# Compression of keys and values with position columns beside raw rows, second layers among other products, and gate rows turned half a chunk later

## The reference

```
kv = (h @ w_kv).reshape(B, T, 6, 4, 64)          # h: tokens normed and modulated, T = 512
k_cmp_raw, v_cmp_raw = kv[:, :, 0], kv[:, :, 1]  # 4 groups of 64
tok = arange(31)[:, None] * 16 + arange(32)      # 31 blocks of 32 tokens, stride 16
def compress(raw, j):
    blk = raw[:, tok] + cmp_pos[j]               # cmp_pos: (2, 32, 64)
    blk = ... .reshape(B, 31, 4, 32 * 64)
    hid = gelu(blk @ cmp_w1[j] + cmp_b1[j])      # (2048 -> 256)
    return hid @ cmp_w2[j] + cmp_b2[j]           # (256 -> 64)
gates = sigmoid((h2 @ w_in)[..., 1024:])         # 48 gates a token: 16 heads x 3 branches
o = gates[0] * o_compressed + gates[1] * o_selected + gates[2] * o_window
```

## Time and profile before

| | |
|---|---|
| time, median of 3 runs | 1574.64 us |
| profiled execution, its own time | 1574.64 us |
| its span in the trace | 1572.9 us |
| PE busy | 1517.3 us (96%) |
| DVE busy | 1101.3 us (70%) |
| ACT busy | 692.1 us (44%) |
| POOL busy | 291.8 us (19%) |

### The profile page before, as it was taken

The page is one execution under the profiler, slowest core; times in us unless marked ns, Lnnn a source line. Parts: engine busy times, 40 slices in busy tenths (PEclk is TensorE's granted clock), DMA queues, the critical chain, the costliest instruction groups (busy, mean ns, idle before and its releaser), DMA issues. The chain is left out here.

```text
span 1572.9 us, 20896 instructions
## 1 busy us (share of the span) xinstructions
PE 1517.3 (96%) x8187; PEld 1258.8 (80%) x8187; DVE 1101.3 (70%) x1610; ACT 692.1 (44%) x1176; POOL 291.8 (19%) x233
## 2 busy tenths in 40 slices
PE   4999999999999999989999999999999999999998
PEld 3888888888888887867777888888888988677677
DVE  6798688889988753458884785656634815888775
ACT  3433551323224543347774632323233525877651
POOL 0200013223231000149872011111100011000210
PEclk9999999999999999999999999999999999999999
DMA  9674267577684215310001164443332232111101
GB/s 332 238 271 165 81 215 248 195 251 255 207 315 134 81 59 168 104 56 2 2 2 41 68 221 161 144 146 119 134 107 90 75 107 93 68 54 54 54 1 54
DMA packets 106744, 203.35 MB, mean 129 GB/s; under 512 B 6025, under 2 KB 11414, under 8 KB 106646
## 3 DMA queue, kind: packets, MB, share of 16 engines
q1 hardware_dynamic: 106646, 202.01, 37.6%
HBM read 199.90 MB, written 2.10 MB: 128 GB/s over the span
## 5 line engine op out<-in xcount | busy, mean ns | idle before, releaser
L727 ACT ACTIVATE WH<-RAW 128x2048 fp32r<-128x2048 f32 (+1 forms) x111 | 208.1, 1886 | 354.9 <-DMA RAW<-in_ff_w_in_dram 223.7
L1242 DVE TENSOR_TENSOR WL<-RAW,WH 128x2048 fp32r<-128x2048 f32 (+1 forms) x107 | 269.1, 2538 | 120.0 <-ACT WH L727 119.2
L491 POOL PARTITION_ALL_REDUCE MROW<-MACC x26 | 123.3, 4744 | 600.8 <-DVE MACC L1276 515.9
L2105 PE MATMUL PS<-WH,HIDh 128*128 128x512 f32 (+1 forms) x576 | 217.4, 377 | 1.1 <-DVEq L1818 1.1
L2105 PE MATMUL PS<-WL,HIDh 128*128 128x512 f32 (+1 forms) x576 | 217.3, 377 | 0.0
L2105 PE MATMUL PS<-WH,HIDl 128*128 128x512 f32 (+1 forms) x576 | 217.3, 377 | 0.0
L2105 PE MATMUL PS<-HTh,WH 128*128 128x512 f32 (+1 forms) x520 | 202.5, 389 | 0.6 <-DVE WL L1242 0.6
L2105 PE MATMUL PS<-HTl,WH 128*128 128x512 f32 (+1 forms) x520 | 202.4, 389 | 0.0
L2105 PE MATMUL PS<-HTh,WL 128*128 128x512 f32 (+1 forms) x520 | 202.3, 389 | 0.0
L1276 DVE SCALAR_TENSOR_TENSOR MACC<-MRAW,CS,MACC 128x512 f32<-128x512 f32 x168 | 126.3, 752 | 8.6 <-DMA MRAW<-in_ada_w_dram 1.1
L2062 PE MATMUL PS<-HTh,WH 128*128 128x256 f32 (+1 forms) x384 | 125.3, 326 | 6.8 <-DVE WL L1242 4.4
(11 more groups left out here) (341 smaller groups left out, 2991.4 us busy)
## 6 DMA issues: line engine op xcount, KB each, us to landing
MRAW<-in_ada_w_dram SPq DMA_DIRECT2D x44, 1024.0 KB, 7.4
RAW<-in_ff_w_in_dram SPq DMA_DIRECT2D x32, 1024.0 KB, 5.4
RAW<-in_ff_w_out_dram SPq DMA_DIRECT2D x32, 1024.0 KB, 5.1
RAW<-in_w_in_dram SPq DMA_DIRECT2D x16, 1024.0 KB, 5.4
MRAW<-in_w_ada_dram SPq DMA_DIRECT2D x12, 1024.0 KB, 8.6
RAW<-in_a_w_in_dram SPq DMA_DIRECT2D x8, 1024.0 KB, 9.9
MRAW<-in_kv_ada_w_dram SPq DMA_DIRECT2D x8, 1024.0 KB, 6.0
RAW<-in_kv_w_dram SPq DMA_DIRECT2D x6, 1024.0 KB, 5.2
```

The costliest lines, as they stand in the source:

```text
L491: pool.partition_all_reduce(MROW[:], MACC[:], P, RADD).then_inc(m_red, 1)
L727: act.activation(WH[:, wslot(u), 0:width(u)], RAW[:, u % 4, 0:width(u)], ACT.Copy).then_inc(w_hi, 1)
L1242: dve.tensor_tensor(WL[:, u % 4, 0:width(u)], RAW[:, u % 4, 0:width(u)], WH[:, wslot(u), 0:width(u)].bitcast(F32), ALU.subtract).then_inc( ...
L2105: mm = pe.matmul(po, a, b_, start=(k == 0 and i == 0), stop=(k == KT - 1 and i == len(ops) - 1), skip_group_check=len(ops) > 3)
```

## The change

- Positions are no longer added to the rows. The raw rows go to a tile RK ordered by offset within a stride (8 offsets), for each of which 128 columns (4 groups of 32) lie side by side, with one position column at each end. The first layer reads 128 columns of it (124 before) for each weight piece; the product of positions arrives in PSUM columns 0 and 128. The 16 adds on DVE and the tile RP go away.
- DVE adds the two position columns and the bias `cmp_b1` with two instructions of one column per hidden half (`hidden_bias`), and the gelu takes the sum as its bias.
- The first layer goes to banks 4 to 7, which the group before the last has freed, so it doesn't wait for group 36 to be read out.
- The order on PE becomes: keys both halves, values first half, second layer of keys, values second half, scores. The second layer of values stands behind the scores of unit 3, and its bias on DVE behind the maximum of unit 5. `vc_copies` is waited for ahead of the first turn (unit 12).
- CW1v is loaded in two DMAs of 128 columns, each with its semaphore.
- The gate rows are turned between the two halves of the next chunk. ACT rounds the next weight halves ahead of the sigmoid.

```diff
+    sb("RK_END", [P, 32])
-    R = at("R", [P, 2, GROUPS, T // 2], F32, o_rb)
+    RK = at("RK", [P, 2, 8, 130], F32, o_rb)
-    RP = at("RP", [P, 2, 2, 8, GROUPS, CMP], F32, o_hid + 16384)
@@ sync_program
-        sp.dma_start(CW1[1][:], cmp_w1[1].rearrange("(m p) n -> p m n", p=P)).then_inc(cw_in, 16)
+        for mo in range(2):
+            s = slice(P * mo, P * mo + P)
+            sp.dma_start(CW1[1][:, :, s], cmp_w1[1].rearrange("(m p) n -> p m n", p=P)[:, :, s]
+                         ).then_inc(cw1_in[mo], 16)
@@ pool_program
         pool.tensor_copy(VC[32:64, :, HD:2 * HD], VC[0:32, :, 0:HD]).then_inc(vc_copies, 1)
+        pool.wait_ge(vc_copies, 1)
@@ act_program
-        chunk(gates)
+        split_next()
+        act.wait_ge(full, 4 * n.group + 1)
+        act.activation(GROW[:], bank(n.group, 0)[0:48, :], ACT.Copy).then_inc(ev_a, 1)
+        n.group += 1
+        n.chunk += 1
+        split_next()
+        act.wait_ge(full, 4 * n.group)
+        act.activation(GT[:].rearrange("p t g -> p (t g)"), bank(n.group - 1, 1)[:, 0:TT * 48], ACT.Sigmoid
+                       ).then_inc(ev_a, 3)
...
-        chunk(halves(raw_kv))
+        chunk(halves(raw_kv), split=False)
...
             for mo in range(2):
-                act.activation(HC[:, mo, :], PS[:, 2 * j + mo, 0:GROUPS * CMP], ACT.Gelu_apprx_tanh,
-                               bias=C1[:, C_B1 + 2 * j + mo:C_B1 + 2 * j + mo + 1]).then_inc(hc_r, 1)
+                act.wait_ge(hc_b, 4 * j + 2 * mo + 2)
+                act.activation(HC[:, mo, :].rearrange("p (g c) -> p g c", c=CMP),
+                               hidden(j, mo)[:, 1:129].rearrange("p (g c) -> p g c", c=32)[:, :, 0:CMP],
+                               ACT.Gelu_apprx_tanh, bias=SM[:, 40 + 2 * j + mo:41 + 2 * j + mo]).then_inc(hc_r, 1)
@@ evict_raw
-            two = ps[HD * e:HD * e + HD, :].rearrange("p (t o) -> p o t", o=2)
+            two = ps[HD * e:HD * e + HD, :].rearrange("p (c m o) -> p o m c", m=8, o=2)
             for odd in range(2):
-                last = copy(R[HD * odd:HD * odd + HD, j, h, :], two[:, odd, :])
+                last = copy(RK[HD * odd:HD * odd + HD, j, :, 1 + 32 * h:33 + 32 * h], two[:, odd])
+    def hidden(j, mo):
+        return PS[:, 4 + 2 * j + mo, :]
@@ dve_program
...
+        def hidden_bias(j, mo):
+            ps, i = hidden(j, mo), 2 * j + mo
+            dve.wait_ge(hc_f, i + 1)
+            b = SM[:, 40 + i:41 + i]
+            dve.tensor_tensor(b, ps[:, 0:1], C1[:, C_B1 + i:C_B1 + i + 1], ALU.add).then_inc(hc_b, 1)
+            dve.wait_ge(hc_b, 2 * i + 1)
+            dve.tensor_tensor(b, ps[:, 128:129], b, ALU.add).then_inc(hc_b, 1)
+        hidden_bias(0, 0)
+        hidden_bias(0, 1)
+        hidden_bias(1, 0)
...
+        hidden_bias(1, 1)
...
+            if t == 5:
+                compressed_values()
@@ pe_program
         pe.wait_ge(t2_rdy, 16)
-        chunk("A", HIDh, HIDl)
+        chunk("A", HIDh, HIDl, between=turn_gates)
...
+        def hidden_rows(j, mo):
+            pe.wait_ge((cw0_in, cw1_in[mo])[j], 16)
+            for m in range(16):
+                half = m // 8
+                mm = pe.matmul(hidden(j, mo)[:, half:half + P], CW1[j][:, m, P * mo:P * mo + P],
+                               RK[:, j, m % 8, 2 * half:2 * half + P], start=(m == 0), stop=(m == 15),
+                               skip_group_check=True)
+            mm.then_inc(hc_f, 1)
+        evicted(35)
+        hidden_rows(0, 0)
+        hidden_rows(0, 1)
+        hidden_rows(1, 0)
+        pe.wait_ge(hc_r, 2)
+        pe.wait_ge(cw_in, 64)
...
+        hidden_rows(1, 1)
+        def compressed_values():
+            pe.wait_ge(hc_r, 4)
...
-        pe.wait_ge(kc_r, 3)
+        pe.wait_ge(kc_r, 2)
...
-        pe.wait_ge(vc_copies, 1)
         for t in range(UNITS + VALUES_LAG):
             if t < UNITS:
                 scores(t)
+            if t == 3:
+                compressed_values()
+            if t == TURN_LAG:
+                pe.wait_ge(vc_copies, 1)
```

More of the change, by code:

```diff
@@ L251, in program @@
     ln_st, ln_sd, ln_v, mix_c = sem("ln_st"), sem("ln_sd"), sem("ln_v"), sem("mix_c")
-    cw0_in = sem("cw0_in")
-    cw_in, rp_c, hc_f, hc_r, kc_f, kc_r = (sem(n) for n in (
-        "cw_in", "rp_c", "hc_full", "hc_rdy", "kc_full", "kc_rdy"))
+    cw0_in, cw1_in = sem("cw0_in"), [sem("cw1_in0"), sem("cw1_in1")]
+    cw_in, hc_f, hc_b, hc_r, kc_f, kc_r = (sem(n) for n in (
+        "cw_in", "hc_full", "hc_bias", "hc_rdy", "kc_full", "kc_rdy"))
     k_hi, k_lo, kc_full32 = sem("k_hi"), sem("k_lo"), sem("kc_full32")
@@ L998, in act_program @@
         for j in range(2):
-            act.wait_ge(hc_f, 2 * j + 2)
-            if j == 1:
-                act.wait_ge(kc_f, 1)
             for mo in range(2):
-                act.activation(HC[:, mo, :], PS[:, 2 * j + mo, 0:GROUPS * CMP], ACT.Gelu_apprx_tanh,
-                               bias=C1[:, C_B1 + 2 * j + mo:C_B1 + 2 * j + mo + 1]).then_inc(hc_r, 1)
+                act.wait_ge(hc_b, 4 * j + 2 * mo + 2)
+                act.activation(HC[:, mo, :].rearrange("p (g c) -> p g c", c=CMP),
+                               hidden(j, mo)[:, 1:129].rearrange("p (g c) -> p g c", c=32)[:, :, 0:CMP],
+                               ACT.Gelu_apprx_tanh, bias=SM[:, 40 + 2 * j + mo:41 + 2 * j + mo]).then_inc(hc_r, 1)
             if j == 0:
@@ L1007, in act_program @@
                 act.wait_ge(pool_c, 8)
-                act.activation(KCF[:, :, 0:CMP], PS[:, 4, 0:GROUPS * CMP].rearrange("p (g c) -> p g c", c=CMP),
+                act.activation(KCF[:, :, 0:CMP], PS[:, 3, 0:GROUPS * CMP].rearrange("p (g c) -> p g c", c=CMP),
                                ACT.Identity,
@@ L1673, in odd_banks, with raw_kv @@
             return evict
-        chunk(odd_banks(lambda b, ps: evict_raw(dve.tensor_copy, ev_d, b, ps)))
+        def raw_kv(b, ps):
+            if b == 1:
+                for half in range(2):
+                    pos = C02[:, P + Q_POS:P + Q_POS + 32].rearrange("p (j a m) -> p a j m", j=2, a=2)[:, half]
+                    dve.tensor_copy(RK[:, :, :, 129 * half], pos)
+            evict_raw(dve.tensor_copy, ev_d, b, ps)
+        chunk(odd_banks(raw_kv))
         def kv_br(br):
@@ L1711, in dve_program @@
         dve.tensor_tensor(KCl[:], KCF[:], KCh[:].bitcast(F32), ALU.subtract).then_inc(kc_r, 1)
[L1712 to L1716, removed]
+        hidden_bias(1, 1)
+        def compressed_values():
+            dve.wait_ge(kc_f, 2)
+            dve.wait_ge(cw_in, 64)
+            dve.wait_ge(vc_zero, 3)
+            dve.tensor_tensor(VC[0:CMP, :, 0:HD], PS[0:CMP, 4, 0:GROUPS * HD].rearrange("p (g d) -> p g d", g=GROUPS),
+                              B2V[:, None, :].to_broadcast([CMP, GROUPS, HD]), ALU.add).then_inc(kc_r, 1)
         def four(t):
@@ L2110, in chunk @@
                     mm.then_inc(w_used, 1)
[L2111 to L2116, removed]
             n.group += 1
@@ L2353, in pe_program, with turn_gates @@
         chunk("G", HTh, HTl, width=48)
+        def turn_gates():
+            g = n.group - 1
+            pe.wait_ge(ev_a, freed(g)[0] + 1)
+            for tt in range(TT):
+                mm = pe.transpose(bank(g, 1)[:, 48 * tt:48 * tt + 48], GROW[:, P * tt:P * tt + P], IDENT[0:48, 0:48])
+            mm.then_inc(full, 3)
         pe.wait_ge(t2_rdy, 16)
-        chunk("A", HIDh, HIDl)
+        chunk("A", HIDh, HIDl, between=turn_gates)
         chunk("A", HIDh, HIDl, mixed=True)
         chunk("A", HIDh, HIDl, mixed=True)
[L2359 to L2372, removed]
-                for mo in range(2):
[L2374 to L2380, removed]
@@ new lines, in pe_program, with compressed_values @@
+        hidden_rows(1, 0)
+        pe.wait_ge(hc_r, 2)
+        pe.wait_ge(cw_in, 64)
+        pe.wait_ge(ev_a, freed(37)[0])
+        pe.wait_ge(ev_d, freed(37)[1])
+        for mo in range(2):
+            mm = pe.matmul(PS[:, 3, 0:GROUPS * CMP], W2K[:, mo].rearrange("p a d -> p (a d)"), HC[:, mo, :],
+                           start=(mo == 0), stop=(mo == 1))
+        mm.then_inc(kc_f, 1)
+        hidden_rows(1, 1)
+        def compressed_values():
+            pe.wait_ge(hc_r, 4)
+            for h in range(GROUPS):
+                for mo in range(2):
+                    mm = pe.matmul(PS[0:CMP, 4, HD * h:HD * h + HD], HC[:, mo, CMP * h:CMP * h + CMP],
+                                   W2V[:, mo, :], start=(mo == 0), stop=(mo == 1))
```

## The result

The changed kernel takes 1563.63 us (median of 5 runs, 1561.35 to 1566.41), the kernel before 1574.64 us. The ratio is 0.9937, 95% interval 0.9925 to 0.9949; a second comparison with more runs gave 1563.77 against 1573.49 us, 0.9939 [0.9925, 0.9953]. So the change takes 9.7 to 11.0 us off, where 9.1 was forecast. The profiled execution took 1565.33 us, its span 1563.6 us.

The account below looks back on a forecast made before the run. PE, busy 96% of the span, was taken as the bound. Its terms summed to -9.98 us, cut to 9.1 by POOL's lateness: 1574.64 - 9.1 = 1565.5 us, range 1561.5 to 1569.5.

Parts of the forecast that it names:

- rival 1: First scores: POOL is not the later one, or the clock stays up; gain 10 to 12 us, chance 0.13.
- The gates: Gate chunk: PE's idle time waiting for ACT's copy of the rows goes, -2.09 us; sigmoid keeps 2.2 us of cover.
- rival 3: Gate chunk: the sigmoid is late, PE waits for its banks, the 2.09 us hole returns; 1567.6 us, chance 0.06.
- First-layer gap and clock: Compression's first layer: starts at once, -2.95 us; without the hole its first 64 instructions run at full clock, -1.63 us.
- Four more columns: First layer: 128 columns per instruction for 124, taken as +0.47 us if columns set the step, 0 if weight load does.
- The second layer of keys and of values: Compression: only keys' second layer stays between first-layer halves, -0.78 us; the stretch before the first score empties, -3.00 us.
- POOL's split: First score: waits for POOL's split queries, ready 16.5 us behind group 36, 0.9 us after PE; gain 9.1 us.
- Rival 4: First score: POOL's code change grows beyond 9.3 us and moves all of attention; at 24 us 1580 us, chance 0.08.
- The weights: CW1v's load in 512 B packets: a wait of 0 to 2 us at the second layer of keys, taken as 0.
- The start of attention: First units' scores: moved second layer of values against a clock that may stay up; bounds -2.3 to +1.5, taken as 0.
- The bound of -2.3 for the clock: Start of attention: most the clock staying up could gain, half of 4.53 us busy at 0.50, 2.3 us.
- the sign for this step: Start of attention: prediction wrong if unit 6's scores come later behind the first score than before; no size given.

Follow-up runs that it names:

- filler: Kernel before with 12 unread products in PE's 2.95 us hole ahead of the first layer; 1573.28 against 1573.41 us (0.9992).
- values_early: Changed kernel with the second layer of values ahead of unit 3's scores, not behind them; 1561.16 against 1573.41 us (0.9924).
- compress_only: Changed kernel with the gate rows turned right behind their products, as before; 1567.83 against 1573.41 us (0.9961).
- table_again: Changed kernel with values' second layer ahead of unit 3's scores and one unread exponential behind the last gelu; 1560.86 against 1573.49 us (0.9923).
- one_dma: Changed kernel with CW1v loaded in one DMA of 1 KB rows and one semaphore; one run, 1568.22 us.
- gates_only: Kernel before with only the gate rows turned half a chunk later; 1567.78 against 1573.41 us (0.9968).
- all_again: As table_again, with an unread one-column add on POOL ahead of its wait for group 36; 1560.19 against 1573.49 us (0.9911).
- after_again: The changed kernel measured once more, unedited, as base of a second comparison; 1563.77 against 1573.49 us (0.9939).
- pool_early: Changed kernel with an unread one-column add on POOL ahead of its wait for group 36; 1561.28 against 1573.18 us (0.9924).
- all_early: Changed kernel with values' second layer ahead of unit 3's scores, unread exponential behind the last gelu, unread early POOL add; 1560.99 against 1573.18 us (0.9925).

## Why the prediction was right, step by step

The forecast of 1565.5 us was right in sign and size (1563.6). The time lies in the stated range, but below the forecast's own band (1564.7 to 1566.5) and in that of rival 1 (1562.5 to 1564.6). The sum was right partly by luck, because two errors nearly cancel: 10.70 us at the first score, where 9.1 was predicted, and 2.40 given back, where 0 was. The 1.6 us more at the first score are POOL's 0.9, the columns' 0.47 and some 0.2 of small differences.

- **The gates: right.** -2.09 predicted; 2.16 us gained when group 36 completes (SP's issue of CW1v moves from 660.44 to 658.85, with the +0.57 taken off). The cover was as worked out: the sigmoid ends at 611.5 (610.9 predicted), PE has no wait for its banks, rival 3 did not come.
- **First-layer gap and clock: right.** No hole, clock 1.00, 64 instructions in 7.31 us (7.38 predicted, had 9.01); `filler` shows that the hole made the slow clock.
- **Four more columns: wrong, a term of +0.47 that is 0.** The step is (665.80 - 658.66) / 64 = 0.112 us with 128 columns. With 124 the second 64 of the trace before took 7.31 us, as the first 64 do now; the forecast's 0.113 and 7.38 came from starts rounded to 0.1 us. Of the two that could have set the step, columns and weight load, the columns were the wrong choice; that the weight load sets it is not shown.

```profile
673.62 7.31 PE L2367 MATMUL PS<-RP,CW1v 128*128 128x124 f32 x64
```

- **The second layer of keys and of values, -0.78 and -3.00: right.** PE ran through to the first score, 15.2 us behind the start of the first layer.
- **POOL's split: mis-sized, the cause right.** I took 9.3 us for the code change from the row of that instruction; it took 8.26 us here, and the three affine selects before it 0.29 to 0.31 us, where two of them took 0.54 and 0.53. The pair is ready 14.8 us behind group 36, and not 16.5: in step with PE. The first half of rival 1 came true. Over ten executions the gap in this place was 8.14 to 10.61 us, so one row was a weak support for a wait of 0.9; `values_early` shows POOL late by 0.28, `compress_only` by 0.40, `table_again` by 0.92 and `one_dma` by 1.00 us. Rival 4's growth did not come, rather the opposite: the six executions with CW1v in 512 B packets had 8.14 to 9.21 us, the four with it in one load of 1 KB packets 9.39 to 10.61. Why was not tried. The figure of about 6 us that the Trainium skill ("GPSIMD Engine Reference", Instruction dispatch) gives, quoted with the forecast, is shorter than all ten.
- **The weights: right, 0.** PE never waits for them. They came at 305 and 291 GB/s, as the row of 512 B packets let expect (296), and `one_dma` shows that a margin this thin needed the split.
- **The start of attention: wrong, the failed step.** 0 was predicted, bounds -2.3 to +1.5; it gave back 2.40 us. Unit 3's scores, which wait for the first exponential, came 4.55 us behind the first score (678.40 - 673.85), where it was 3.76 before: 1.03 us for the subtraction beside POOL, less 0.24 for faster products (`gates_only` has 3.52 there in the old order, at a clock of 1.00). I had moved POOL's second pair of splits beside DVE's chain and costed it as PE's wait alone. From there to unit 7 it took 5.66 us for 4.04, because the second layer of values, 16 instructions, stands on PE at the low clock: 1.84 us (679.43 to 681.27), and not 1.08. And the clock did not stay up: before, PE's slow products had filled the time until the exponential (idle 0.97 us); fast ones left a hole of 2.87 us, and the clock fell behind that instead. The bound of -2.3 for the clock was too wide as well: `gates_only` and `filler`, in the old order and at 1.00 behind the first score, reach unit 7 in 7.03 us for 7.80, 0.8 us less, because PE then waits 1.83 us for the exponential and the clock falls behind that wait (to 0.66 in `gates_only`). `all_again` gets to 5.86 us, with three more edits.

```profile
682.28 0.60 PE L2405 MATMUL PS<-KC,QS 128*128 128x64 f32 x4 [1.24 <-POOL VC L565]
...
685.80 0.51 PE L2417 MATMUL PS<-KDh,QS 128*128 128x512 f32 x1 [1.83 <-ACT PBC L1018]
...
689.32 1.04 PE L2405 MATMUL PS<-KC,QS 128*128 128x64 f32 x4
```

The prediction had named the sign for this step: unit 6's scores later behind the first score than before. They came 8.78 us behind it (682.63 - 673.85), where it was 6.71 (690.69 - 683.98). The rows are those of before and of after:

```profile
690.69 0.67 PE L2414 MATMUL PS<-KDh,QS 128*128 128x512 f32 x1
```

```profile
682.63 0.47 PE L2451 MATMUL PS<-KDh,QS 128*128 128x512 f32 x1
```

The time is 9.7 to 11.0 us lower and the stage explains 8.3 to 8.5; what is left is within what the clock at the three places can take, 1.6 us each, and isn't shown to be the change's.

## What to carry to other kernels

When holes of a busy engine are closed, follow the next wait at the new speed: work that ran slowly had covered a wait, and moved work belongs into the hole that opens, ahead of the instruction that waits, and not behind it. Setup costs (a table load, POOL's code change) can be drawn forward by one tiny unread operation, where the trace shows them on a chain behind a wait. Compare traces at the end of the stage that was changed, since a later stage can differ by several us from one execution to the next.

## What was not expected of the hardware

- The 128x128 subtraction on DVE: 0.29 us alone, 1.32 beside POOL's two-operand operation. The key split of the same size had 1.27 us before, where POOL's split had started 0.14 us earlier. It takes 0.29 us after, where it starts 0.06 us ahead of POOL's (671.01), and 1.35 us in `after_again`, where it starts 0.06 us behind POOL's (670.64). The one that starts first is held up little: POOL's at 671.01 took 1.36 us, that at 670.64 took 1.26. The rows are of after and of `after_again`:

```profile
670.95 0.29 DVE L1729 TENSOR_TENSOR KC<-KCF,KC 128x128 fp32r<-128x128 f32 x1
```

```profile
670.70 1.35 DVE L1729 TENSOR_TENSOR KC<-KCF,KC 128x128 fp32r<-128x128 f32 x1
```

- A hole's length alone does not tell the clock behind it: 1.85 us in `pool_early` left 1.00, 1.86 us in `values_early` was followed by 0.61. The same hole differs too: 1.13 to 1.15 us a little behind unit 7 left 1.00 in eight traces, and 0.53 to 0.61 in `compress_only`, `one_dma` and `table_again`. The rows are of `pool_early` and `values_early`:

```profile
676.40:680.50 4.10, 3.48 (x28) 2.32 (x28) 2.47 (x6) 2.88 (x11) 0.05 (x1) 1.00 0.00 0
```

```profile
678.40:681.90 3.50, 3.50 (x12) 2.10 (x12) 2.39 (x5) 2.90 (x11) 0.00 (x0) 0.61 0.00 0
```

- POOL's gap before its first two-operand addition: 8.14 to 10.61 us in the same place of ten executions, 8.84 to 9.50 where `pool_early`, `all_early` and `all_again` drew it forward to about 502.
